# Grouped-query attention: reciprocal softmax sums spread through a row in DRAM instead of by TensorE, with the division two steps behind the weighted values

## The reference

```
q, k = rms_norm(q, q_norm_w), rms_norm(k, k_norm_w)      # then rotary positions for the latent tokens
p = softmax(q k^T * 64**-0.5)                            # latent: 1024 own keys + 128 cached; context: its 128 own
o = p v                                                  # then o @ w_o_gqa, gate, residual
```

## Time and profile before

| what | us |
|---|---|
| median of 3 runs | 3579.81 (3578.88 to 3584.06) |
| profiled execution, its own time | 3582.87 |
| its span in the trace | 3581.1 |
| TensorE matmul busy | 3333.6 (93%) |
| VectorE busy | 1872.2 (52%) |
| ScalarE busy | 1185.4 (33%) |
| GpSimd busy | 941.1 (26%) |

### The profile page before, as it was taken

One profiled execution on the slowest core, in us unless ns is written; L12 is line 12 of the kernel. 1 busy time (PEld: TensorE's weight loads), 2 busy tenths in 40 slices (PEclk: granted clock), 3 DMA queues, 4 the chain that ended last, 5 costly groups with the idle time before them and its releaser, 6 DMA issues. The chain is left out here.

```text
span 3581.1 us, 51581 instructions
## 1 busy us (share of the span) xinstructions
PE 3333.6 (93%) x20797; PEld 3080.1 (86%) x20797; DVE 1872.2 (52%) x2655; ACT 1185.4 (33%) x2106; POOL 941.1 (26%) x726
## 2 busy tenths in 40 slices
PE   5999999997999999999979999999798999999997
PEld 4777777785989999999978777777698999999996
DVE  4556565554165545555454555565326555555455
ACT  3344444444132121222233555555423121221212
POOL 1122222122333222332242122221133222322221
PEclk8999999997999999999999999999899999999998
DMA  6333333323311111111112111101321111111101
GB/s 245 97 95 107 104 110 97 110 69 113 100 42 53 42 41 35 41 48 46 36 57 67 33 26 35 29 22 33 124 74 59 42 42 35 41 51 43 35 30 59
DMA packets 206659, 229.78 MB, mean 64 GB/s; under 512 B 30564, under 2 KB 173533, under 8 KB 205341
## 3 DMA queue, kind: packets, MB, share of 16 engines
q1 hardware_dynamic: 186973, 162.69, 14.9%
q10 hardware_dynamic: 11664, 42.47, 3.6%
q0 software_dynamic: 7856, 22.29, 1.7%
HBM read 181.79 MB, written 31.98 MB: 60 GB/s over the span
## 5 line engine op out<-in xcount | busy, mean ns | idle before, releaser
L205 PE MATMUL psum<-Hh,wh 128*128 128x384 f32 x3360 | 1142.9, 340 | 49.8 <-ACT Hh L377 11.3
L206 PE MATMUL psum<-Hh,wl 128*128 128x384 f32 x3360 | 1131.4, 337 | 0.0
L207 PE MATMUL psum<-Hl,wh 128*128 128x384 f32 x3360 | 1131.3, 337 | 0.0
L286 DVE SCALAR_TENSOR_TENSOR x<-psum,mod,x 128x384 f32<-128x384 f32 (+2 forms) x768 | 377.4, 514 | 684.7 <-PE psum L207 643.5
L205 PEld LDWEIGHTS psum<-Hh,wh 128*128 128x128 f32 x3360 | 637.3, 190 | 60.3 <-issue 35.3
L206 PEld LDWEIGHTS psum<-Hh,wl 128*128 128x128 f32 x3360 | 637.3, 190 | 0.0
L207 PEld LDWEIGHTS psum<-Hl,wh 128*128 128x128 f32 x3360 | 637.0, 190 | 0.0
L816 POOL TENSOR_TENSOR wl<-wr,wh 128x1024 fp32r<-128x1024 f32 x88 | 219.9, 2498 | 986.5 <-ACT wh L735 986.5
L766 ACT ACTIVATE ff_u<-psum 128x768 f32<-128x768 f32 x88 | 71.6, 814 | 1109.2 <-PE psum L207 1109.2
L205 PE MATMUL psum<-ff_ah,ff_dh 128*128 128x384 f32 x1056 | 365.2, 346 | 29.4 <-POOL ff_al L838 20.7
L964 DVE SCALAR_TENSOR_TENSOR ff_c<-ff_u,par,ff_c 128x1153 f32<-128x1153 f32 x176 | 377.4, 2144 | 15.8 <-DVE ff_c L961 5.2
(11 more groups left out here) (217 smaller groups left out, 4244.4 us busy)
## 6 DMA issues: line engine op xcount, KB each, us to landing
wr<-w_up SPq DMA_DIRECT2D x88, 512.0 KB, 3.9
ff_dr<-w_down SPq DMA_DIRECT2D x22, 1024.0 KB, 6.0
da_mw<-mod_w ACTq DMA_DIRECT2D x40, 512.0 KB, 3.9
wr<-mod_w ACTq DMA_DIRECT2D x40, 512.0 KB, 4.8
wr<-w_qkv_diff SPq DMA_DIRECT2D x24, 512.0 KB, 19.5
x<-x_save SPq DMA_DIRECT2D x16, 576.0 KB, 7.3
in_mw<-mod_w SPq DMA_DIRECT2D x8, 1024.0 KB, 12.3
Hh<-oh_save SPq DMA_DIRECT2D x14, 576.0 KB, 9.6
```

The lines of the kernel that those rows point to most:

```text
L205: pe.matmul(out, w_hi, m_hi, start=start, stop=False)
L206: pe.matmul(out, w_lo, m_hi, start=False, stop=False)
L207: return pe.matmul(out, w_hi, m_lo, start=False, stop=stop)
L286: last = dve.scalar_tensor_tensor(g.x[:, m, lo:hi], g.PS[:, bank, lo - n * NB:hi - n * NB], g.mod[:, gate + m, cond:cond + 1], g.x[:, m, l ...
```

## The change

TensorE no longer spreads the reciprocals. `sums` writes them to one of two buffers, ordered by half and tile. SP (`spread_sums`) stores a buffer to a small DRAM tensor so that each tile's 128 reciprocals lie in one row, waits for the landing, and loads the rows back, repeated over the 64 partitions of each half, into one of two buffers `rb`. ScalarE copies only the weighted values; `divide` multiplies them with `rb`. The divisions of the first three pairs are made in steps 4, 6 and 8, ahead of the rotary instructions there, those of the last two in steps 0 and 1 of the next head. In SP's list a spread of the first pair stands between a head's weight load and its query swap, the other four behind the swap; the first out weights stand behind the first spread of head 7, and `load_outputs` behind its last.

```diff
--- before.py
+++ after.py
@@ -152,6 +152,7 @@
         g.lam = sb("lam", [P, 4])
         g.Hh = sb("Hh", [P, KC, T], F32R)
         g.Hl = sb("Hl", [P, KC, T], F32R)
+        g.rl_rows = nc.dram_tensor("rl_rows", [2, 2, 2, P], F32, kind="Internal").ap()
         g.x_save = nc.dram_tensor("x_save", [P, KC, T], F32, kind="Internal").ap()
         g.wr = sb("wr", [P, 2, KC, P])
         g.wh = sb("wh", [P, 2, KC, P], F32R)
@@ -1741,6 +1742,7 @@
 
 
 PAIR_AT = {2: 0, 4: 1, 6: 2, 8: 3, 9: 4}
+DIVIDE_AT = {4: 0, 6: 1, 8: 2}
 
 
 def gqa_filler(j, s):
@@ -1846,17 +1848,13 @@
         "cos": ([P, NS], F32), "sin": ([P, NS], F32), "q": ([P, T], F32), "rot": ([P, NS], F32), "sq": ([P, T], F32),
         "nqh": ([P, 2, T], F32R), "nql": ([P, 2, T], F32R), "nkh": ([P, 2, KW], F32R), "nkl": ([P, 2, KW], F32R),
         "v": ([P, 2, KW // P, P], F32), "e": ([P, 2, NKEY], F32), "pt": ([P, 2, TT, 2 * P], F32),
-        "yb": ([P, 2, 2 * P], F32), "y": ([P, 2, 2 * P], F32), "yh": ([P, 2 * P], F32R), "yl": ([P, 2 * P], F32R),
-        "nm": ([P, 2], F32), "nb": ([P, 2], F32), "l": ([P, 4, 2], F32), "rl": ([P, 2, 2], F32), "wq": ([P, 1], F32),
+        "yb": ([P, 2 * P], F32), "rb": ([P, 2, 2 * P], F32), "y": ([P, 2, 2 * P], F32), "yh": ([P, 2 * P], F32R), "yl": ([P, 2 * P], F32R),
+        "nm": ([P, 2], F32), "nb": ([P, 2], F32), "l": ([P, 4, 2], F32), "rl": ([P, 2, 2, 2], F32), "wq": ([P, 1], F32),
         "ms": ([P, TT, 2], F32), "rk": ([P, 2, TT, 2], F32), "r": ([P, 2, TT, 2], F32)},
         "tab w_in0 w_in1 w_hi w_lo free0 free1 full free2 free3 free4 ahead side sq_d ck_in ck_d cv_in ko_d v_st k_st ms_d r_d normed kswap swap rope"
-        " s_mm mx nmax exp rl_d pv_out y_d y_split y_out wq_d wo_in0 wo_in1 wo_hi wo_lo o_in")
+        " s_mm mx nmax exp rl_d rl_out rl_in pv_out y_d y_split y_out wq_d wo_in0 wo_in1 wo_hi wo_lo o_in")
     free = {"F": b.free0, "C": b.free1, 0: b.free2, 1: b.free3, 2: b.free4}
     w_in = [b.w_in0, b.w_in1]
-    BC0 = 2 * P
-
-
-
     early = b.pt[:, :, :, :].rearrange("p m c q -> p (m c q)")
     k = [early[:, p * KW:(p + 1) * KW] for p in range(2)]
     vt = [early[:, 2 * KW:2 * KW + T], early[:, 0:T]]
@@ -1920,6 +1918,22 @@
                 ring.wait_read(sp, free, ("vt", p, 2))
                 for m in range(2):
                     sp.dma_start(a.new_v_gqa[0, 0, 2 * p + m], b.v[:, p, KW // P - 1, m * DH:(m + 1) * DH]).then_inc(b.v_st, 16)
+
+            def spread_sums(j, p):
+
+                n, done = PAIRS[p][1], len(PAIRS) * j + p
+                sp.wait_ge(b.rl_d, done + 1)
+                if done >= 2:
+                    sp.wait_ge(b.rl_in, 32 * (done - 1))
+                rows = g.rl_rows[done % 2]
+                sp.dma_start(rows.rearrange("m i q -> q (m i)"), b.rl[:, done % 2, :, :].rearrange("p m i -> p (m i)"),
+                             allow_slow_non_contiguous=True).then_inc(b.rl_out, 16)
+                if done >= 2:
+                    sp.wait_ge(b.y_d, done - 1)
+                sp.wait_ge(b.rl_out, 16 * done + 16)
+                for m in range(2):
+                    sp.dma_start(b.rb[m * DH:(m + 1) * DH, done % 2, 0:n * P],
+                                 rows[m, 0:n].rearrange("i q -> (i q)").partition_broadcast(DH)).then_inc(b.rl_in, 16)
 
             load_w(("K", 1))
             load_w(("V", 0))
@@ -1944,11 +1958,15 @@
             for j in range(HEADS):
                 if j + 3 < HEADS:
                     load_w(("Q", j + 3))
+                spread_sums(j, 0)
                 if j + 1 < HEADS:
                     swap_queries(j + 1)
-            sp.wait_ge(b.w_lo, len(UNITS) - 2)
-            sp.wait_ge(b.full, ring.done(("Q", HEADS - 1, NN - 1)))
-            first_out_weights(g, sp, b, 1)
+                for p in range(1, len(PAIRS)):
+                    if (j, p) == (HEADS - 1, 1):
+                        sp.wait_ge(b.w_lo, len(UNITS) - 2)
+                        sp.wait_ge(b.full, ring.done(("Q", HEADS - 1, NN - 1)))
+                        first_out_weights(g, sp, b, 1)
+                    spread_sums(j, p)
             sp.wait_ge(b.y_out, 32 * len(PAIRS) * (HEADS - 1) + 16)
             load_outputs(g, sp, b)
             sp.wait_ge(b.o_in, OUT_LOADS)
@@ -2027,8 +2045,7 @@
                     act.wait_ge(b.full, ring.done(use))
                     if done:
                         act.wait_ge(b.y_d, done)
-                    act.activation(b.yb[:, :, 0:n], ring.bank(g, use).rearrange("p (a t) -> p a t", a=2)[:, :, 0:n],
-                                   ACT.Copy).then_inc(free[ring.place[use]], 1)
+                    act.activation(b.yb[:, 0:n], ring.bank(g, use)[:, 0:n], ACT.Copy).then_inc(free[ring.place[use]], 1)
 
             act.wait_ge(b.wq_d, 1)
             for n in range(2):
@@ -2199,16 +2216,12 @@
                 use, (t0, n) = ("PV", j, p), PAIRS[p]
                 out = ring.bank(g, use)
                 ring.wait_free(pe, free, use)
-                pe.wait_ge(b.rl_d, len(PAIRS) * j + p + 1)
-                for i in range(n):
-                    broadcast_heads(g, pe, out[:, BC0 + i * P:BC0 + (i + 1) * P], b.rl[:, i, :])
                 if p == 0 and j % 4 == 0:
                     pe.wait_ge(b.cv_in, 16 * 4)
                 t, nk = t0 + n - 1, keys(t0) // P
                 for c in range(nk):
-                    if nk == 1:
-                        ring.wait_read(pe, free, ("T", j, t, 0, 0))
                     if c % 3 == 0:
+                        ring.wait_read(pe, free, ("T", j, t, 0, c // 3))
                         ring.wait_read(pe, free, ("T", j, t, 1, c // 3))
                     for m in range(2):
                         last = pe.matmul(out[m * DH:(m + 1) * DH, 0:n * P], b.v[:, j // 4, value_chunk(t0, c), m * DH:(m + 1) * DH],
@@ -2313,14 +2326,18 @@
             def sums(j, p):
                 t0, n = PAIRS[p]
                 dve.wait_ge(b.exp, 2 * (TILES * j + t0 + n))
-                dve.reciprocal(b.rl[:, 0:n, :], b.l[:, t0 % 4:t0 % 4 + n, :]).then_inc(b.rl_d, 1)
+                done = len(PAIRS) * j + p
+                if done >= 2:
+                    dve.wait_ge(b.rl_out, 16 * (done - 1))
+                dve.reciprocal(b.rl[:, done % 2, :, 0:n], b.l[:, t0 % 4:t0 % 4 + n, :].rearrange("p i m -> p m i")).then_inc(b.rl_d, 1)
 
             def divide(j, p):
                 n, done = PAIRS[p][1] * P, len(PAIRS) * j + p
                 ring.wait_read(dve, free, ("PV", j, p))
+                dve.wait_ge(b.rl_in, 32 * (done + 1))
                 if done >= 2:
                     dve.wait_ge(b.y_split, 2 * (done - 1))
-                dve.tensor_tensor(b.y[:, done % 2, 0:n], b.yb[:, 0, 0:n], b.yb[:, 1, 0:n], ALU.mult).then_inc(b.y_d, 1)
+                dve.tensor_tensor(b.y[:, done % 2, 0:n], b.yb[:, 0:n], b.rb[:, done % 2, 0:n], ALU.mult).then_inc(b.y_d, 1)
 
             dve.tensor_scalar(b.wq[:, :], g.par[:, PC_QN:PC_QN + 1], SCALE, None, ALU.mult).then_inc(b.wq_d, 1)
             dve.wait_ge(b.tab, 16)
@@ -2361,12 +2378,14 @@
                         maxima(j, s)
                     if s == TILES and j + 1 < HEADS:
                         maxima(j + 1, 0)
-                    for use in gqa_previous(j, s):
-                        if use[0] == "PV":
-                            divide(*use[1:])
+                    if s in DIVIDE_AT:
+                        divide(j, DIVIDE_AT[s])
+                    if s < 2 and j:
+                        divide(j - 1, 3 + s)
                     if j + 1 < HEADS and s in ROPE_AT:
                         rope(("Q", j + 1), ROPE_AT[s])
-            divide(HEADS - 1, len(PAIRS) - 1)
+            for p in (3, 4):
+                divide(HEADS - 1, p)
 
 
 # ---- launch: one core; inputs and outputs as the reference has them ----
```

## The result

The changed kernel takes 3640.28 us (median of 4 runs, 3636.08 to 3646.59), the kernel before beside it 3581.93 (4 runs): a ratio of 1.0172, 95% interval 1.0159 to 1.0185, 58 us slower by the medians and 62 by the ratio. A second set of runs on another occasion gave 3626.99 beside 3581.99, ratio 1.0132 (1.0114 to 1.0150). The forecast was 3586.5, its range 3576 to 3597: the sign was right, the size wrong by 40 to 54 us.

A forecast was written before the change was run, and what follows sets the result against it. TensorE's matmul stream, busy 93% of the span, was taken as the bound. Losses of 18.1 us (end loads) and 0.9 (out weights) less 12.5 gained in heads gave +6.5 us on 3579.81: forecast 3586.5 us, range 3576 to 3597.

The forecast's parts named there:

- SP's queue: SP's in-order DMA list: each spread's store lands in 3.0 us, bounds 1.5 and 6, delaying instructions behind it.
- Rival (b): Spread's store is slow: each us above 3.0 costs 1 us at the end; at 6 us, 3592.5; chance 0.16.
- A store over 6 us: Sign listed as showing the forecast wrong; the spread's store had been put at 3.0 us.
- In heads 0 to 6 it is hidden: A spread takes some 3.0 + 0.9 us and the loads' landing; the division comes over 12 us later, so no cost.
- rival (d): Spread not hidden, divisions hold up VectorE; needs over 12 us per spread; given no chance of its own.
- only hazard: ScalarE's copy of weighted values: its wait for the division is met, every division being ahead of the next pair's copy.
- The end: Stage's closing barrier: saved outputs' loads, queued behind the last spread, delay the out projection by 18.1 us, bounds 16.5 and 21.
- The first out weights: Head 7: loads queued behind the first spread make ScalarE stand 2 us; the chain loses about 0.9 us (0 to 3).
- The terms of the heads: All heads' attention steps: TensorE's savings, VectorE and GpSimd contention and head 3's recovery sum to a 12.5 us gain, bounds 7 and 22.
- TensorE's gain of 15.7: Attention heads: dropping the broadcast matmuls saves 0.49 us for each of 8 x 4 pairs, at most 15.7 us.
- charge whoever starts second: Steps 4 and 6: overlapping VectorE and GpSimd two-input work delays the later starter; gains 4.3 us better without it.
- The 2.2 us for head 3's product: Head 3: GpSimd's weight split starts later, so the rotary product returns from 3.41 to 1.23 us; gain 2.2 (0 to 4.1).

The follow-up runs named there:

- e1: The changed kernel with each store's reciprocals written as 128 pieces of 16 bytes in place of 512 of 4 bytes; 3582.76 us, ratio to the kernel before 1.0014.
- e10: The changed kernel with the 512 four-byte pieces of a store spaced 64 bytes apart in DRAM, loads reading another input; 3584.36 us, ratio 1.0000.
- e12: The changed kernel storing reciprocals to SBUF rows, first out weights moved into head 6, saved outputs' loads before head 7's second spread; 3571.16 us, ratio 0.9965.

## Why the prediction was wrong

**The step that failed: "SP's queue", the store.** "I take 3.0 us, nearer the row with many pieces, bounds 1.5 and 6." It takes about 10, outside both bounds. The rows it was read from the earlier trace rows show pieces of 256 B and more, and the text said that four-byte pieces may cost more than any piece shown; then it bounded them by twice the value all the same. Rival (b) followed that bound to 3592.5 and no further. "A store over 6 us" stood among the prediction's own signs of being wrong.

**"In heads 0 to 6 it is hidden" failed with it.** One spread, 11 us to its loads and 3.4 us of landing, barely fits in two steps. Two in a row do not: in the kernel before, the fourth and fifth reciprocals of head 1 come 8 us apart (2111.19 and 2119.13), and the next head's first reciprocal, behind the fifth division's new place, at 2136.03. The working asked how long one spread takes, not how often the queue gets one. And it gave the loads no price of their own, while a fifth store that goes out right behind the fourth's loads holds them up in some heads, for up to 12.6 us. Together this was rival (d), named with its point ("over 12 us per spread") and given no chance; it is what happened, in some heads of each execution and not in all.

**The single buffer's "only hazard"**, ScalarE's wait for the division, "is met": false once divisions are late (ScalarE 29.6 us in 7 waits), though two buffers gained 7 us at most.

**TensorE's clock** stands nowhere in the working. It took the lost time to be the time that TensorE stands; the matmuls behind a stall run at the lower level for a while, and by the estimate above that is 12 us of what heads 0 to 7 lost.

**The end** was right as a mechanism: +28.3 where 18.1 was said, of which 7.7 is the slower store, 0.9 its later start, 1.3 the loads and 0.4 issues and barrier. With the quick store of e1 it is +16.5. **The first out weights**: right in kind, 8.6 us of ScalarE's wait in place of 2, by the same 7 us of store.

**The terms of the heads** were off one by one. TensorE's gain of 15.7 was too high (10, at most 14). The contention was charged 5.5 us and cost about 1: the rule "charge whoever starts second" is not what the traces show, since in steps 6 and 8 both slow down and GpSimd more, and in step 4 the splits are over before the product starts. (Its working also starts GpSimd 0.08 us early, against rows 4; that changes nothing.) The 2.2 us for head 3's product belong to a thing that comes and goes by itself. The errors offset each other: -12.5 was said for all heads, and e1 shows -9.8 and -1.6, which is luck.

**The rule on small pieces.** The store's pieces are the same 4 bytes in after and in e10, and SP waits 9.5 and 1.6 us for them. The Trainium skill (DMA: Bandwidth & Descriptors, Specifications) has transfers below 512 B done as read-modify-write; that may lie behind the slow neighbours, which no run shows, but by e10 smallness alone does not make a store slow. Its account of one DMA (the same page, Anatomy of one DMA), which is of one issued by GpSimd, puts most of a fixed cost of some 2 us into the receipt of the write. The stores of e1 and e10, issued by SP, agree in size (waits of 1.5 and 1.6 us); in after the time between the last packet and the landing, with idle DMA engines, grows to some 8 us.

## What to carry to other kernels

Where an operation appears nowhere in the trace, its bound has to come from the arithmetic of what breaks at each value, not from doubling the nearest row: here the question "from what price on does it not fit between two uses?" gave 10 us, and the forecast should have carried a real chance there. Count a queue's work per period as well as per item, and look at what is issued right behind a load that somebody waits for. Read a difference between two traces with the granted clock of the same stretch beside it, and against a trace of the same instructions. And before an edit is credited with a gain, run the unedited kernel again beside it, above all where the loss sits in waits that depend on how transfers meet.

## What the runs showed of the hardware

- 512 four-byte pieces side by side in DRAM land about 10 us after the issue, though their packets are taken in under 2 us; 64 bytes apart SP waits 1.6 us, as for 128 pieces of 16 bytes (1.5).
- Loads of 64 KB, with such a slow store issued 1.2 or 1.3 us behind them on the same queue, came in 8.8 to 12.6 us behind their issue in 18 of 64 cases, shortly before the store; with the store held back until they had landed, in at most 5.0 us (16 of 16).
- After TensorE had stood 7.36 us (to 2138.37), the same matmuls started 0.32 us apart in place of 0.17, at a granted clock of 0.50 in place of 1.00, until about 2144.
- GpSimd's two-input splits of 0.61 and 0.73 us take 1.06 to 1.72 when VectorE runs two-input instructions beside them, VectorE's 1.22 and 1.36 us then 1.52 and 1.65. Beside GpSimd's weight split of 2.35 us VectorE's 1.23 us took 3.41 to 4.03 in some traces, in e1 although it had started 0.49 us first; in head 1 of before it took 1.23 and the split 3.03.
- GpSimd's drain at the barrier took 5.85 us before and after, and in e1, e10 and e12.
- A store of 2 KB behind 14 loads of 576 KB on the same queue took 19.5 us.
- The same kernel took 3640.28 us in one set of runs and 3626.99 in another, intervals apart, while the kernel before stayed at 3582.
